# Three small statistics tiles moved to the end of SBUF, so that most working tiles start 1,152 bytes earlier

## The reference

```
# first block
x += rmsnorm(parallel_mixer(rmsnorm(x)))          # 31-tap depthwise conv branch + 8-head GQA with rope, w_in 1024x1792
x += rmsnorm(memory_cross_attention(rmsnorm(x)))  # 4 heads over 256 memory rows
x += rmsnorm(conv_gated_ffn(rmsnorm(x)))          # 1024 -> 2*2816 -> 3-tap conv -> gelu*val -> 1024
# second block, two layers
for i in range(2):
    x += 0.5 * swiglu(rmsnorm(x))                 # 1024 -> 2*2816 -> 1024
    x += pool_mixer(rmsnorm(x)) if i == 0 else mla_mixer(rmsnorm(x))   # MLA: 8 heads of 192/128
    x += 0.5 * swiglu(rmsnorm(x))
```

## Time and profile before

| what | value |
|---|---|
| median of 3 runs | 2582.91 us |
| the three runs | 2585.77, 2582.91, 2579.71 us |
| profiled execution, its own time | 2585.77 us |
| its span, first to last instruction | 2584.5 us |
| mean granted TensorE clock | 0.989 |
| TensorE matmuls busy | 2540.1 us, 98% |
| VectorE busy | 1218.3 us, 47% |
| ScalarE busy | 933.2 us, 36% |
| GpSimd busy | 615.6 us, 24% |
| DMA, mean over the span | 88 GB/s |

### The profile page before, as it was taken

The page is one execution under the profiler, slowest core; times in us unless marked ns, Lnnn a source line. Parts: engine busy times, 40 slices in busy tenths (PEclk is TensorE's granted clock), DMA queues, the critical chain, the costliest instruction groups (busy, mean ns, idle before and its releaser), DMA issues.

```text
span 2584.5 us, 28793 instructions
## 1 busy us (share of the span) xinstructions
PE 2540.1 (98%) x11694; PEld 2087.8 (81%) x11694; DVE 1218.3 (47%) x1611; ACT 933.2 (36%) x1372; POOL 615.6 (24%) x469
## 2 busy tenths in 40 slices
PE   8999999999999999999999999999999999999999
PEld 7777777788887888888888888888888787888887
DVE  5896565555635333335333333333336566433332
ACT  4486343344423333224332222223224454423321
POOL 3663302222203222111222111222101431222200
PEclk9999999999999999999999999999999999999999
DMA  4211312333232233222323333333232111233332
GB/s 169 74 42 57 98 41 66 98 98 98 92 98 79 91 98 95 95 92 81 103 95 97 93 97 96 98 98 96 90 100 79 48 44 47 93 98 98 96 98 92
DMA packets 66484, 227.28 MB, mean 88 GB/s; under 512 B 7216, under 2 KB 8752, under 8 KB 66352
## 3 DMA queue, kind: packets, MB, share of 16 engines
q1 hardware_dynamic: 66352, 225.44, 27.7%
HBM read 223.31 MB, written 2.10 MB: 87 GB/s over the span
## 4 chain that ended last, share of the span: by engine, by line
PE 92%; DVE 4%; ACT 2%; issue 1%; POOL 0%; DMA 0%; SPq 0%; DVEq 0%; ACTq 0%; POOLq 0%
PE main L384 20%; PE main L386 19%; PE main L385 19%; PE score L384 7%; PE score L386 6%; PE score L385 6%; PE out L384 3%; PE out L385 3%; PE out L386 3%; DVE wl L376 1%; PE main L2017 1%; DVE tmp L1331 1%; PE turn L454 0%; PE turn L453 0%; PE turn L1011 0%
## 5 line engine op out<-in xcount | busy, mean ns | idle before, releaser
L376 DVE TENSOR_TENSOR wl<-raw,wh 128x1024 fp32r<-128x1024 f32 (+1 forms) x431 | 561.9, 1305 | 806.4 <-ACT wh L368 805.5
L368 ACT ACTIVATE wh<-raw 128x1024 fp32r<-128x1024 f32 (+1 forms) x431 | 439.9, 1024 | 609.6 <-PE main L386 490.0
L384 PE MATMUL main<-hxh,wh 128*128 128x512 f32 x1208 | 475.8, 394 | 7.7 <-DVE tmp L671 4.2
L386 PE MATMUL main<-hxh,wl 128*128 128x512 f32 x1208 | 472.4, 391 | 0.0
L385 PE MATMUL main<-hxl,wh 128*128 128x512 f32 x1208 | 472.3, 391 | 0.0
L384 PE MATMUL main<-hh,wh 128*128 128x512 f32 x880 | 342.6, 389 | 1.9 <-POOL hl L1572 0.9
L385 PE MATMUL main<-hl,wh 128*128 128x512 f32 x880 | 342.4, 389 | 0.0
L386 PE MATMUL main<-hh,wl 128*128 128x512 f32 x880 | 342.3, 389 | 0.0
L384 PEld LDWEIGHTS main<-hxh,wh 128*128 128x128 f32 x1208 | 228.3, 189 | 60.4 <-DVE tmp L671 4.3
L384 PE MATMUL score<-hxh,wh 128*128 128x512 f32 x664 | 261.3, 394 | 6.4 <-DVE wl L376 4.8
L386 PEld LDWEIGHTS main<-hxh,wl 128*128 128x128 f32 x1208 | 228.1, 189 | 48.0
(11 more groups left out here) (424 smaller groups left out, 3425.7 us busy)
## 6 DMA issues: line engine op xcount, KB each, us to landing
raw<-in_wts SPq DMA_DIRECT2D x375, 512.0 KB, 3.6
raw<-in_wts SPq DMA_DIRECT2D x52, 384.0 KB, 3.1
x<-in_xT SPq DMA_DIRECT2D x4, 512.0 KB, 8.2
out<-x SPq DMA_DIRECT2D x8, 256.0 KB, 3.9
memx<-in_memT SPq DMA_DIRECT2D x1, 1024.0 KB, 9.6
raw<-in_wts SPq DMA_DIRECT2D x4, 256.0 KB, 2.6
band<-in_pool SPq DMA_DIRECT2D x1, 768.0 KB, 4.4
rope<-in_rope SPq DMA_DIRECT2D x1, 512.0 KB, 7.1
```

The costliest lines, as they stand in the source:

```text
L368: e.activation(wh[i % NCONV][:, 0:n], raw[i % NRAW][:, 0:n], ACT.Copy).then_inc(*sig.up("weight_high", ("high", i)))
L376: e.tensor_tensor(wl[i % NCONV][:, 0:n], raw[i % NRAW][:, 0:n], f(wh[i % NCONV][:, 0:n]), ALU.subtract) \
L384: e.matmul(o, ah, bh, start=start, stop=False)
L386: return e.matmul(o, al, bh, start=False, stop=stop)
```

## The change

The ring of four `stat` tiles had three of its members between the stage area and `hxh`, and the fourth at the very end. Now all four lie at the end:

```
@@ -241,7 +241,6 @@
         x = new("x", [P, KC, S])
         base = Map.top
         Map.top = base + STAGE
-        stat_slots = [Slot(new("stat", [P, 96])) for _ in range(3)]
         hx_at = Map.top
         hxh = new("hxh", [P, KC, S], F32R)
         y_at = Map.top
@@ -263,7 +262,7 @@
         acc = new("acc", [P, S])
         sq_slots = [Slot(new("sq", [P, S])) for _ in range(3)]
         tmp_slots = [Slot(new("tmp", [P, S])) for _ in range(5)]
-        stat_slots.append(Slot(new("stat", [P, 96])))
+        stat_slots = [Slot(new("stat", [P, 96])) for _ in range(4)]
         assert Map.top <= 229344, Map.top
```

## The result

The changed kernel takes 2599.67 us at the median of 4 runs (2595.47 to 2600.72), the kernel before 2582.80 us in the same comparison (2579.71 to 2585.77). The ratio on record is 1.0063, with a 95% interval of 1.0051 to 1.0076. (Ratios here are those on record; they are worked out from the runs and need not be the quotient of the two medians to the last digit.) That is 16.9 us more, and slower well beyond the 0.2% that can be told from no change. The forecast was no change, and the range ended at 2590 us: it was wrong.

A forecast was written before the change was run, and what follows sets the result against it. TensorE was taken to bound the kernel, busy 2540.1 of 2584.5 us. All terms were 0 except -0.2 us for DMA at the start, so 2582.91 - 0.2 = 2582.7 us against the median; range 2575 to 2590 us.

The forecast's parts named there:

- The bound: Whole kernel: TensorE sets the time, busy 2540.1 of 2584.5 us, with matmuls 92% of the chain.
- TensorE's moving and stationary operands: All 512-column products, 9,192 matmuls: moving tiles from 128 to 0 modulo 256 costs 0.
- The upper bound of 20 us: Products where both operands move: at most +3 ns (394 against 391) over 6,552 matmuls, +20 us.
- The collision rival: Down products: weight load gives way to the stream and outgrows the step; 13 ns x 2,640 = 34 us, 2617 us; chance 0.05.
- My argument against it: Down products: a unit's eight weight blocks already lie at eight different distances from the stream, with one step for all.
- The cheaper step: Rival, 9,192 matmuls: rounder starts save fetch cycles of the fixed 13 ns; one 3.8 us, two 7.7 us; two or more: 0.05.
- The other terms: Weight split, vector-side tiles and stat tiles cost 0; DMA gains 0.2 us at the start.
- its bound of a tenth: First transfer on the chain, 6.86 us: a gain of at most a tenth, -0.7 us.
- The effect of 3%: First transfer into raw: a 4,096-byte row needs 128 beats instead of 132 when starting at a multiple of 256.
- The clock: Rival: slow-clock spells come or go, 3 us either way; with measurement spread, chance 0.05 each side of going beyond 0.2%.
- The rows that I named for it: Profile rows from 50 to 230 us: granted clock 0.94, some 22 us at 1.2 GHz, said to follow waits of TensorE.

The follow-up runs named there:

- the first map: Only matmuls on constant tiles, 48 in a row per distance between streamed and stationary tile, not the kernel; mean step 226.9 ns at distance 0, 232.5 at 128.

## Why the prediction was wrong, point by point

- **The bound** was right. TensorE's pace sets the time, it waits no more than before, and the loss is all in the step of a matmul.
- **The step that failed is "TensorE's moving and stationary operands", where I took 0.** It measured 17.1 us. I sorted the rows by where each tile starts, and looked for an effect of the start. What counts is the distance of two tiles. By that measure the rows could not show anything: `kn` (73,024) and `qn` (81,216) are 8,192 apart, `kp` and `qp`, `hxh` and `wh`, `hh` and `wh`, `ckl` and `wh` are apart by multiples of 256 as well. All my "alignments" 64 and 128 were one and the same distance, 0 modulo 256. The upper bound of 20 us held the loss, but on the wrong matmuls: I put it on the 6,552 in which both operands move, which did not change at all, and counted the 2,640 in which one moves as free. The 216 of `cqh` and `cql` were in no count.
- **The rows that did hold a distance** were the loads of the second `mv` buffer, at 0, beside `pt` at 64. I read the length of the load there. It says nothing: in the changed kernel loads still take 188 ns, and the step grew all the same. The steps of those products are too few and too mixed to read.
- **The collision rival** had the right place, pair and count, 2,640 matmuls of the down products, and got a chance of 0.05. Its mechanism was half wrong: the load does not have to outgrow the step, it costs the stream some 6.5 ns while its own record stays the same. Its size was therefore twice too large, 34 us against 17.
- **My argument against it failed too.** "Eight blocks at eight distances, one step for all" is true, but the blocks are 512 bytes apart, a multiple of the period. So it could only exclude that multiples of 512 bytes matter.
- **The cheaper step** didn't come: no distance tried at 512 columns has a mean step under 226.7 ns, and moving both operands together changes nothing.
- **The other terms held.** The split takes 1.32 us on DVE and 1.05 on ACT as before, squares take 631 to 632 ns, and PE's waits are those of the earlier trace rows. The first transfer on the chain after, `2.16 6.29 DMA raw<-in_wts`, took 6.29 instead of 6.86 us, within its bound of a tenth. But the other profiles show that this is scatter: with `raw` at 128 it took 6.86, 6.19, 6.13, 6.59 and 7.02 us, with `raw` at 0 6.29, 6.35 and 6.95. The effect of 3% that I estimated from the Trainium skill (DMA: Bandwidth & Descriptors, "How a descriptor splits into AXI transactions") would be lost in this, so that rule is neither shown nor refuted here. The page tells it of bytes that are fetched, while `raw` is a destination.
- **The clock** couldn't do it: it only blurs single profiles by some 7 us, and the four runs of each kernel don't overlap. The rows that I named for it, show the granted clock of a stretch and not what went before its falls.

## What to carry to other kernels

When a change moves tiles, list the pairs that TensorE reads together, the stream and the weights, and compare their distance modulo 256 bytes before and after; 0 was the fastest in long rows of 512-column matmuls with 128 columns of weights, but gained nothing at 256 columns or with 64 columns of weights, and was not enough by itself in groups of three. Ask of every row used as a bound whether it differs in the quantity that might matter, or only in one that looks like it. When TensorE is busy at 100% and the time still grows, count the matmuls in a stretch or take the distance of starts: neither the waits, nor the chain, nor the weight loads show a slower stream; the mean record of the group does, by 6 ns.

## What the runs showed of the hardware

- In a row of like ones, a 512-column float32r matmul with its load of 128x128 weights has a step of 226.7 ns if stationary and moving tile start at the same byte modulo 256, and 228 to 234 ns otherwise, even at a difference of 4 bytes. At 256 columns and a distance of 128 there is no such loss, nor with 64 columns of weights. Between other matmuls, the step was 231 ns at distance 0.
- At one wrong distance the steps are not equal but repeat a pattern; for 128 bytes in the first map they run from 228 to 241 ns, with seven steps to a period.
- If only one weight tile of three is at another distance, two of the three steps are slow: 226.7 + 232.7 + 234.0 = 693.4 ns for the three, against 680 ns with none and 697 ns with all three far. One stray tile costs four fifths of what three cost there. In the whole kernel it was 13.2 ns for the three, against 19.5 with all three far: two thirds.
- The Trainium skill, SBUF — State Buffer, section "Who interferes with whom", gives TensorE two independent read ports, one for the moving operand and one for the weights. The steps above differ from what independence would give, and the measurement decides: where the two operands lie to each other changes the pace.
- The load's own record at full clock is 187 to 189 ns for 128 columns of weights at every distance, with some at 192. What in the reads gives this period, and which of the two loads around a stream it meets, was not settled.
